# Third expert's up weights kept outside the ring, in descriptor space and in the residual's place, with a new order of the expert stage's first turns

## The reference

```python
g_prob = softmax(t @ w_group + b_group); g_idx = argmax(g_prob)        # 4 groups
e_prob = softmax(e_logits of that group)                              # 8 experts a group
top_p, top_i = top_k(e_prob, 2)
gate = g_w * top_p / sum(top_p)
# for each of 32 experts e, on the tokens that chose it:
hb = silu(xb @ w1[e]) * (xb @ w3[e])        # 1024 -> 512, twice: "up"
y  = hb @ w2[e]                             # 512 -> 1024: "down"
x  = x + segment_sum(y * gate)
```

## Time and profile before

| what | value |
|---|---|
| median of 3 runs | 1962.44 us (1959.52 to 1962.62) |
| the profiled execution: time, span | 1959.95 us, 1958.2 us |
| TensorE busy | 1821.1 us, 93% |
| VectorE, ScalarE, GpSimd busy | 659.2, 402.0, 165.9 us |
| DMA moved | 489.30 MB, mean 250 GB/s |
| expert weights | 195 loads of 2048.0 KB |
| mean granted clock of TensorE | 0.991 of full speed |

### The profile page before, as it was taken

How to read it: one execution, slowest core, us unless ns; L and a number is a source line. 1 busy time by engine, 2 the same in 40 slices (tenths; PEclk the granted TensorE clock), 3 DMA queues, 4 the chain that set the end, 5 groups by cost and what they waited for, 6 DMA issues and landing times. The chain is left out here.

```text
span 1958.2 us, 24605 instructions
## 1 busy us (share of the span) xinstructions
PE 1821.1 (93%) x10238; PEld 922.9 (47%) x10238; DVE 659.2 (34%) x1235; ACT 402.0 (21%) x773; POOL 165.9 (8%) x212
## 2 busy tenths in 40 slices
PE   7989999999999999998699999999989999999976
PEld 4435875454444443333253469544554444334422
DVE  6357547136311111110243575531471111111112
ACT  3121345144100000000112324431530000000001
POOL 3000000003100000000300000000030000000002
PEclk9999999999999999999899999999999999999999
DMA  9502103321999999999650110062058999999996
GB/s 371 193 1 44 23 10 129 129 87 58 395 427 427 427 427 428 429 426 428 256 206 1 33 23 13 13 254 84 27 232 349 427 427 427 428 428 428 428 428 228
DMA packets 87810, 489.30 MB, mean 250 GB/s; under 512 B 45384, under 2 KB 50248, under 8 KB 60064
## 3 DMA queue, kind: packets, MB, share of 16 engines
q1 hardware_dynamic: 80288, 471.12, 58.8%
q0 software_dynamic: 7424, 16.78, 2.3%
HBM read 464.29 MB, written 31.98 MB: 253 GB/s over the span
## 5 line engine op out<-in xcount | busy, mean ns | idle before, releaser
L2024 PE MATMUL bank<-ring,hT 128*64 128x512 f32 x2080 | 472.4, 597 | 39.0 <-DMA ring<-in_we 33.3
L2024 PEld LDWEIGHTS bank<-ring,hT 128*64 128x64 f32 x2080 | 141.4, 137 | 321.3 <-issue 248.4
L2031 PE MATMUL bank<-ring,arena 128*64 128x512 f32 x1040 | 238.3, 600 | 19.0 <-DVE arena L2551 9.7
L1000 PE MATMUL bank<-hT,ring 128*128 128x512 f32 (+1 forms) x576 | 253.3, 600 | 0.0
L1000 PEld LDWEIGHTS bank<-hT,ring 128*128 128x128 f32 (+1 forms) x576 | 109.1, 190 | 140.5 <-issue 139.2
L2009 PE MATMUL bank<-shift_in,arena 128*128 128x256 bf16 (+2 forms) x1632 | 171.0, 262 | 0.0
L2009 PEld LDWEIGHTS bank<-shift_in,arena 128*128 128x128 bf16 x1632 | 140.8, 98 | 62.7 <-issue 48.7
L2070 DVE TENSOR_TENSOR hT<-bank,colp 128x512 f32<-128x512 f32 (+1 forms) x68 | 45.5, 669 | 342.9 <-PE bank L2009 340.0
L2382 ACT ACTIVATE arena<-bank 128x256 f32<-128x256 f32 x65 | 25.0, 384 | 644.1 <-PE bank L1995 644.1
L2031 PEld LDWEIGHTS bank<-ring,arena 128*64 128x64 f32 x1040 | 71.3, 137 | 153.3 <-issue 135.3
L2041 POOL DMA_INDIRECT expert_rows<-arena,row_places x64 | 62.7, 979 | 874.4 <-DVE arena L2546 874.4
(11 more groups left out here) (469 smaller groups left out, 1975.2 us busy)
## 6 DMA issues: line engine op xcount, KB each, us to landing
ring<-in_we SPq DMA_DIRECT2D x195, 2048.0 KB, 23.7
ring<-in_w_in SPq DMA_DIRECT2D x6, 2048.0 KB, 19.1
expert_rows<-ring SPq DMA_DIRECT2D x1, 8448.0 KB, 24.4
ring<-in_w_out SPq DMA_DIRECT2D x4, 2048.0 KB, 10.2
ring<-in_wm SPq DMA_DIRECT2D x2, 2048.0 KB, 8.3
ring<-in_w_in SPq DMA_DIRECT2D x2, 1920.0 KB, 16.4
ring<-in_w_in SPq DMA_DIRECT2D x2, 1664.0 KB, 26.9
ring<-in_w_in SPq DMA_DIRECT2D x2, 1152.0 KB, 28.6
```

What stands on the lines that cost most here:

```text
L1000: last = nc.tensor.matmul(B[n % 4][0:w, :], ins_units[unit][:, k, u0:u0 + w], hT[:, k, :], start=k == 0, stop=k == KD - 1)
L2024: last = nc.tensor.matmul(bank[CAP * j:CAP * j + CAP, :], x[:, k, :], up_w(u, j, k), start=k == 0, stop=k == KD - 1)
L2031: last = nc.tensor.matmul(bank[CAP * half:CAP * half + CAP, :], hid[u][:, m, :], down_w(slot, m, half), start=m == 0, stop=m == HM - 1)
```

## The change

What it does:

1. `dynamic_dma_scratch_size` goes from 16384 to 4096 bytes, and the 12288 bytes become `ahead`, 3072 numbers a partition.
2. Before the stage's first product SP loads the first half of expert 2's up weights into `ahead` and into `lora_w` and `gup_w`, parameters that are not read again in this layer. It writes `xT` to DRAM (`residual_aside`), waits for that, and for the flips and squares that read `xT`, and loads the second half over `xT`. Only the 88 other loads go to the ring; expert 4's up weights come into places 0 and 1 where expert 2's came.
3. At the end of SP's list, in both layers, `xT` is loaded back and SP waits for the landing. In the last layer this stands behind the wait for `store_extra`.
4. TensorE's first turns: flip 0 stands before the second half of expert 1's up product, and down 0 and flip 1 before the gather of experts 2 and 3.
5. VectorE: the copy of the ranks and `gather_first(0)` stand before the two `select`; the first `gate_out` and `rows_out` stand before `gather_first(1)`; the slots' steps stand behind `tokens(0, 0, 0)`.
6. GpSimd: `token_rest(0)` waits for `s_sel`, the first selection.

```diff
+        xs_d = nc.dram_tensor("residual_aside", (P, KD * SEQ), F32, kind="Internal").ap()
+        ahead = sb("ahead", [P, 3072])
+            x_flat = xT[:, :, :].rearrange("p k t -> p (k t)")
+            ahead_w = [ahead[:, DE * z:DE * z + DE] for z in range(6)] + [lora_w[:, :], gup_w[:, :]]
+            def third_w(j, k):
+                return ahead_w[4 * j + k] if k < 4 else x_flat[:, 2048 * j + DE * (k - 4):2048 * j + DE * (k - 3)]
...
                     for j in range(2):
                         load_unit(eng, 1, j, 1, s_e[3 + j])
+                    third_up = [we_d[expert_row(2), :, j, :].rearrange("a p n -> p (a n)") for j in range(2)]
+                    eng.dma_start(ahead[:, :], third_up[0][:, 0:3072]).then_inc(s_x1, 16)
+                    eng.dma_start(lora_w[:, :], third_up[0][:, 3072:3584]).then_inc(s_x1, 16)
+                    eng.dma_start(gup_w[:, :], third_up[0][:, 3584:4096]).then_inc(s_x1, 16)
                     eng.wait_ge(s_o, 2 * KD)
                     load_unit(eng, 1, 2, 1, s_e[5])
+                    eng.wait_ge(s_or, 2 * KD)
+                    eng.dma_start(xs_d, x_flat).then_inc(s_xw, 16)
+                    eng.wait_ge(s_xw, 16)
+                    eng.wait_ge(s_ht, 2 * NT)
+                    eng.wait_ge(s_sq, 2 * KD)
+                    eng.dma_start(x_flat, third_up[1]).then_inc(s_x2, 16)
...
-                        if ups:
+                        if ups and start != 1:
...
-                            if start == 0:
-                                eng.wait_ge(s_ua, 3)
-                                load_unit(eng, 0, 0, 4, s_e[0])
...
                     eng.wait_ge(s_ua, 1)
-                    load_unit(eng, 0, 0, 2, s_e[0])
+                    load_unit(eng, 0, 0, 4, s_e[0])
                     eng.wait_ge(s_mu, 1)
-                    load_unit(eng, 0, 1, 2, s_e[1])
+                    load_unit(eng, 0, 1, 4, s_e[1])
...
+                    eng.wait_ge(s_mu, 3)
+                    eng.dma_start(x_flat, xs_d).then_inc(s_xb, 16)
+                    eng.wait_ge(s_xb, 16)
                     for z in range(2):
                         eng.wait_ge(s_yo[z], 16 * (NE // 2) * (layer + 1))
...
+                    eng.wait_ge(s_sel, 1)
                     token_rest(0)
...
-    nc = _bacc.Bacc("TRN2", target_bir_lowering=False, num_devices=1)
+    nc = _bacc.Bacc("TRN2", target_bir_lowering=False, num_devices=1, dynamic_dma_scratch_size=4096)
```

More of the change, by code:

```diff
@@ L2235, in up @@
                         w = u % 2
-                        eng.wait_ge(s_e[3 * w + half], 32 * g + 16 * (u // 2 + 1))
-                        pe_up_half(w, xgg[z][:, :, CAP * u:CAP * u + CAP], half, b_up[w]).then_inc(
+                        third = isinstance(g, int) and g == 0 and u == 2
+                        if third:
+                            eng.wait_ge((s_x1, s_x2)[half], (48, 16)[half])
+                        elif w == 0 and not (isinstance(g, int) and g == 0):
+                            eng.wait_ge(s_e[half], 32 * g + 16 * (u // 2))
+                        else:
+                            eng.wait_ge(s_e[3 * w + half], 32 * g + 16 * (u // 2 + 1))
+                        pe_up_half(w, xgg[z][:, :, CAP * u:CAP * u + CAP], half, b_up[w], third).then_inc(
                             (s_ua, s_mu)[half], 1)
@@ L2293, in _ @@
                     up(0, 0, 1, 0)
-                    up(0, 0, 1, 1)
                     eng.wait_ge(s_ys, 2)
                     flip(0, 0)
+                    up(0, 0, 1, 1)
+                    down(0, 0)
+                    flip(0, 1)
                     eng.wait_ge(s_h3, 2 * NT)
@@ L2304, in _ @@
                     up(0, 0, 2, 0)
-                    down(0, 0)
                     gather(0, 0, 0)
-                    flip(0, 1)
                     eng.wait_ge(s_tk, 4)
@@ L2507, in _, with rows_out, gate_out, tokens @@
                     eng.sem_inc(s_ml, 1)
+                    def rows_out(g, u):
+                        w = u % 2
+                        eng.wait_ge(s_dn, GE * g + (u + 1))
+                        if not (isinstance(g, int) and g == 0 and u < 2):
+                            eng.wait_ge(s_yo[w], 32 * g + 16 * (u // 2) + yo_done)
+                        eng.tensor_copy(ysb[w], b_down[w][:, :]).then_inc(s_ys, 1)
+                    def gate_out(g, u):
+                        w = u % 2
+                        eng.wait_ge(s_sg, GE * g + (u + 1))
+                        eng.tensor_tensor(hid[w], sg[w], up_half(b_flip[w], 1), ALU.mult).then_inc(s_hd, 1)
+                    def tokens(g, z, u, ranks):
+                        gather_out(GE * g + (GE + u + 1), 1 - z, u, group_width(g + 1))
+                        if u == 0 and ranks:
+                            select(eng, z, rankm[:, bass.ds(GE * (g + 2), GE), :]).then_inc(s_sel, 1)
+                    def turn(g, z, u, more, ranks):
+                        if more and u == GE - 1:
+                            tokens(g, z, u, ranks)
+                        gate_out(g, u)
+                        if more and u < GE - 1:
+                            tokens(g, z, u, ranks)
+                        rows_out(g, u)
+                    gate_out(0, 0)
+                    eng.wait_ge(s_h3, 2 * NT)
+                    rows_out(0, 0)
                     gather_first(1)
+                    gate_out(0, 1)
+                    tokens(0, 0, 0, True)
                     if FINAL:
```

53 lines of the change are left out of this document (17 added, 36 removed).

## The result

The changed kernel takes 1969.12 us (median of 20), the kernel before 1962.53 us (median of 20): a ratio of 1.0029, interval 1.002 to 1.0039. That is slower by 5.7 us by the ratio, between 3.9 and 7.6; the two medians lie 6.6 apart. The profiled execution took 1966.26 us, 6.31 more than the profiled one of before.

The account below looks back on a forecast made before the run. It took the expert stage to be bound by its loads, with SP waiting for free ring places; 0.0 - 4.4 + 1.9 + 7.6 = +5.1 us on 1962.4 gave 1967.5 us, 8-in-10 range 1962.5 to 1971.

Parts of the forecast that it names:

- The loads bound, and the 4 MB are worth nothing as placed: Expert stage: full ring places leave the queue idle from about 512 to 526 us, so two fewer ring loads gain nothing.
- Layer 0's first turns, 0.0: Layer 0's stage start: earlier start, new waits, down 1 ending at 526.25, down 3 landing at 533.95 against 534.0: 0.0 us.
- rival 3: Longer waits before flip 0 lower the clock, selects wait for GpSimd: +7 to +10 us, 1969.5 to 1972; 16%.
- The selections hold GpSimd: Layer 0's first turns: the two selects on VectorE hold GpSimd in full, 2.35 us, delaying the copy-out before flip 0.
- Layer 1, -4.4: Layer 1's first turns: the 5.83 us wait before down 0 goes, down 3 lands at 1489.75 against 1494.2: -4.4 us.
- Layer 1's end, +7.6: Layer 1's end: the residual is loaded after store_extra landed, alone on an idle queue: +7.6 us.
- Layer 0's end, +1.9: Layer 0's end: the last store lands with the residual, GpSimd's drain ends at 959.2: +1.9 us, nothing if the store overtakes.
- it comes from the clock: Rival stated before the experiments, whole kernel: the time comes from the granted clock; no size or chance given.

Follow-up runs that it names:

- experiment 3: The kernel before with parts 1 to 3 of the change (the loads) and the old order of turns: 1972.74 us, ratio 1.0052 to before.
- experiment 4: experiment 1 with expert 5's up weights also loaded outside the ring once expert 2's are used, residual returning after them: 1952.54 us, ratio 0.9953 to before.
- experiment 5: The changed kernel with the places outside the ring reused by experts 2, 5, 8 and 11, residual back after expert 11's up products: 1938.69 us, ratio 0.9884 to before.
- experiment 1: The changed kernel with the last layer's residual load issued right behind the last ring load, ahead of store_extra: 1959.99 us, ratio 0.9993 to before.
- experiment 8: The changed kernel without GpSimd's wait for s_sel ahead of its first token part: 1972.02 us, ratio 1.0049 to before.
- experiment 6: The changed kernel with the two selects moved behind the first gate_out on VectorE: 1960.43 us, ratio 1.0008 to before.
- experiment 2: The kernel before with parts 4 to 6 of the change (orders on TensorE, VectorE, GpSimd), all loads as before: 1961.62 us, ratio 1.0 to before.
- experiment 9: Both kernels, unaltered, profiled two more times each: the kernel before 1958.78 and 1957.81 us, the changed kernel 1968.89 and 1971.69 us.
- before again: The kernel before, unaltered, profiled a second time: 1958.78 us.
- experiment 7: experiment 5 with the two selects moved as in experiment 6: 1937.46 us, ratio 0.9877 to before.

## Why the prediction was right, and where it was not

The forecast was 1967.5 us, +5.1 against before; measured +5.7 (1969.1 us). Point by point:

- **The loads bound, and the 4 MB are worth nothing as placed:** shown. Hole from 515 to 526 (forecast 512 to 526; down 2 took 10.9 us to land and not 8), down 3 lands at 534.2, and experiments 3, 4 and 5 give the same edit no gain, a gain of 7.9 and a gain of 21 us (by the ratios, the last two against experiment 1; in the stages themselves 5.2 and 17.9), by what they do to the holes.
- **Layer 0's first turns, 0.0:** +0.2 at down 3. The start is right and GpSimd's wait is its cause (experiment 8). The waits are right in their sum only: 4.0 and 1.2 were forecast, measured are 3.04, 0 and 1.6 us of work at the low clock, so that down 1 ends at 526.1 (forecast 526.25). The low clock is what rival 3 had named. In layer 0 it cost nothing of its own: VectorE's list work ended at 499.7 and `gate_out` at 500.3, and down 0 at 500.4 would have waited for it anyway. In layer 1 it was the same, `gate_out` ending at 1458.5 and down 0 starting at 1458.7.
- **The selections hold GpSimd:** shown by experiment 6, for 1.8 us, not the 2.35 "in full" that I had taken. The Trainium skill, "SBUF — State Buffer", section "Who interferes with whom", has the two shut each other out; that both lose time here (3.65 against 2.35, 4.10 against 2.32 us) agrees.
- **Layer 1, -4.4:** measured -4.4, from the issue of expert 1's down weights to the landing of down 3. Experiments 2 and 3 add that neither half of the change gives it alone: from that issue to the last expert landing they have 1.1 us less than before and 0.4 more, the changed kernel 3.9 less.
- **Layer 1's end, +7.6:** 7.8, and experiment 1 takes it away. The Trainium skill's "DMA: Bandwidth & Descriptors", section on the anatomy of one DMA, would give 6.8, an estimate by its figures for the gpsimd path. Measured are 7.7 to 7.9, 0.1 to 0.3 more than SP's row of before (7.6) had it.
- **Layer 0's end, +1.9:** this term was mis-sized. The block ended 1.1 us later; the store did wait for the residual (4.5 us instead of 2.3), but GpSimd's drain came closer behind it. And the next block then started 1.7 us earlier than before: TensorE's branch behind the block took 0.44 us, against 3.42 before. In the three executions of before it took 3.42, 0.44 and 2.54, so part of this is chance.
- **Missing from the sum:** the second block ahead of its experts, whose code the change does not touch, +4.1 in the profiled pair and 4.1 to 7.5 over three. This is the part of the rival "it comes from the clock" that holds (experiment 9). I had looked at the clock only where the change moves TensorE's waits. So the right total owes something to luck: up to the second block's start the profiled pair stands 3.6 us under the forecast's terms (-1.7 where +1.9 was forecast, in part by a branch that varies), the second block is 4.1 over them, and the two cancel. Without the second block the pair differs by 2.2 us. The rest of the terms stand on rows of their own.

## What to carry to other kernels

In a stage bound by transfers, weights kept outside the buffer buy time only if the transfer queue has a free place to go on with; follow the first load that is issued late, and find which product releases its place. The same 4 MB of places brought nothing when used once and 22 us against before when reused until the queue had no hole. A transfer that restores something should be issued behind the last load of the stage and not behind its last store.

## What the runs showed of the chip that I had not expected

- Writing 2 MB of SBUF to DRAM took 13.6 us (460.4 to 474.0), the first 8.7 of them beside a load that took 9.5 instead of 7.6. The second half over it took 7.8, and SP, free from 474.3, had its next issue at 484.8: none of it was on the path.
- A wait of TensorE of 3.0 to 3.1 us ahead of flip 0 was followed by a fall of the clock in both layers of the changed kernel and of experiments 1, 2, 4 and 5; waits of 1.3 and 2.71 us there (experiments 6, 7 and 8) were not. One of 3.35 us was in one kernel and not in the other, and the 2.3 us wait at the routing's end was in one of three executions of the kernel before (experiment 9, "before again", at 473.8) and not in the other two. So the length of a wait alone does not say it.
- The branch behind layer 0's expert block took TensorE about 0.4 us or 2.5 to 3.9 us, from kernel to kernel and from execution to execution; what decides it was not looked for.
